# The end of the down projection: a turned tile copied between its sums, PSUM copies between squares, the fourth Winograd sum ahead of the corner

## The reference, cut to what matters

```python
for i in range(DEPTH):                       # DEPTH = 2
    u = rms_norm_2(h, mix_pre_g[i])
    # layer 0: dilated attention, layer 1: differential attention; both begin with u @ w_in
    h = h + rms_norm_2(y, mix_post_g[i])
    # ... attention to a memory, in the same form ...
    u = rms_norm_2(h, ffn_pre_g[i])
    y = swiglu_ffn(u, w_gate_up[i], w_down[i])       # (silu(g) * up) @ w_down
    h = h + rms_norm_2(y, ffn_post_g[i])

def rms_norm_2(x, g):
    y = xf * lax.rsqrt(jnp.mean(xf * xf, axis=-1, keepdims=True) + EPS)
    return (y * g).astype(x.dtype)
```

## Time and profile before

| | us |
|---|---|
| median of 3 runs | 3115.54 |
| lowest, highest | 3115.42, 3120.82 |
| profiled execution, its own time | 3113.84 |
| its span | 3112.0 |
| PE busy in the span | 2887.1 (93%) |
| DVE busy | 1111.0 (36%) |
| ACT busy | 667.3 (21%) |
| POOL busy | 508.7 (16%) |

### The profile page before, as it was taken

How to read it: one execution, slowest core, us unless ns; L and a number is a source line. 1 busy time by engine, 2 the same in 40 slices (tenths; PEclk the granted TensorE clock), 3 DMA queues, 4 the chain that set the end, 5 groups by cost and what they waited for, 6 DMA issues and landing times.

```text
span 3112.0 us, 32431 instructions
## 1 busy us (share of the span) xinstructions
PE 2887.1 (93%) x12564; PEld 1910.6 (61%) x12564; DVE 1111.0 (36%) x2286; ACT 667.3 (21%) x1512; POOL 508.7 (16%) x777
## 2 busy tenths in 40 slices
PE   8999998889999987899999999999798899999998
PEld 4465543244655432387656488888585554688887
DVE  3534311135343111334621243354346722333354
ACT  3332210023232100102621211100204622211100
POOL 2001111121021111112310012100113610011201
PEclk9999999999999999999999999999899999999999
DMA  3113599941116999622021122222121021122122
GB/s 146 48 48 148 211 394 410 415 168 48 48 64 225 388 417 414 243 82 81 1 79 57 54 82 82 82 75 102 54 82 55 1 81 54 54 85 106 68 75 88
DMA packets 121906, 421.35 MB, mean 135 GB/s; under 512 B 9232, under 2 KB 13456, under 8 KB 95504
## 3 DMA queue, kind: packets, MB, share of 16 engines
q1 hardware_dynamic: 108528, 383.62, 32.3%
q0 software_dynamic: 12640, 33.45, 2.9%
q10 hardware_dynamic: 576, 2.10, 0.2%
HBM read 408.64 MB, written 27.26 MB: 140 GB/s over the span
## 4 chain that ended last, share of the span: by engine, by line
PE 79%; DMA 10%; DVE 4%; ACT 2%; issue 2%; DVEq 1%; POOLq 0%; POOL 0%; SPq 0%; ACTq 0%
PE ps L2359 31%; PE ps L406 13%; DMA ring_feat<-in_w 7%; PE ps L2593 6%; PE ps L1591 4%; PE ps L1071 4%; PE ps L2613 4%; PE ps L1631 2%; PE ps L2467 2%; PE ps L2839 2%; DMA big<-in_w 2%; PE ps L1843 1%; PE ps L1854 1%; PE ps L1866 1%; PE ps L2684 1%
## 5 line engine op out<-in xcount | busy, mean ns | idle before, releaser
L406 PE MATMUL ps<-ring_feat 128*96 128x512 f32 (+3 forms) x768 | 308.5, 558 | 11.0 <-DVE tmp L465 4.4
L2359 PE MATMUL ps<-big 128*128 128x256 f32 x1200 | 268.1, 379 | 0.0
L2359 PE MATMUL ps<-ring_feat 128*128 128x256 f32 x1152 | 262.3, 379 | 0.0
L2359 PEld LDWEIGHTS ps<-big 128*128 128x128 f32 x1200 | 228.0, 190 | 31.0
L406 PEld LDWEIGHTS ps<-ring_feat 128*128 128x128 f32 (+1 forms) x768 | 140.6, 186 | 163.6 <-issue 122.1
L2359 PEld LDWEIGHTS ps<-ring_feat 128*128 128x128 f32 x1152 | 218.9, 190 | 30.6 <-issue 1.0
L2593 PE MATMUL ps<-ring_feat 128*128 128x512 f32 x448 | 194.6, 593 | 2.9 <-ACT ring_feat L2739 2.2
L1591 PE MATMUL ps<-big,tmp 128*64 128x512 f32 x512 | 123.7, 632 | 33.7 <-DMA big<-in_w 30.7
L1591 PE MATMUL ps<-ring_feat,tmp 128*64 128x512 f32 x512 | 123.8, 632 | 28.4 <-DMA ring_feat<-in_w 26.4
L2593 PEld LDWEIGHTS ps<-ring_feat 128*128 128x128 f32 x448 | 84.2, 190 | 106.7 <-issue 101.9
L1606 DVE TENSOR_TENSOR tmp<-tmp,ps 128x256 f32<-128x256 f32 x32 | 13.5, 421 | 328.0 <-ACT tmp L1600 328.0
(11 more groups left out here) (467 smaller groups left out, 4506.4 us busy)
## 6 DMA issues: line engine op xcount, KB each, us to landing
big<-in_w SPq DMA_DIRECT2D x48, 2048.0 KB, 17.5
ring_feat<-in_w SPq DMA_DIRECT2D x48, 2048.0 KB, 14.9
ring_feat<-in_w_gate_up SPq DMA_DIRECT2D x22, 2048.0 KB, 8.0
ring_feat<-in_w_mix_in SPq DMA_DIRECT2D x12, 2048.0 KB, 8.1
ring_feat<-in_w_down SPq DMA_DIRECT2D x12, 1536.0 KB, 6.7
tmp<-in_w_mem_kv SPq DMA_DIRECT2D x6, 2048.0 KB, 20.5
ring_feat<-in_w_out SPq DMA_DIRECT2D x4, 2048.0 KB, 8.6
big<-expert_out SPq DMA_DIRECT2D x16, 512.0 KB, 7.9
```

The source lines that it names most:

```text
L406: yield T.matmul(bank, lhs(k), rhs(k), start=k == 0, stop=k == n - 1)
L2359: m = T.matmul(to, lhs[:, j, :], rhs[:, j, :], start=start and j == 0, stop=stop and j == chunks - 1)
```

## The change

The last read-out of the down projection is written in another order, and one POOL sum changes place.

In the Winograd sums (both `mix_group` and the down projection) U4 comes ahead of C22 on POOL. U4 is now written over U2 where it was written over P5, so that C22 can still read P5; the drain between the two is gone. DVE's corner C12 reads U4 there. Waits for the last of POOL's sums name C22 now.

`down_read` and the calls of `add_tile` become one function, `down_outputs`, that writes each engine's list for both groups. In the first half nothing but U4's place is different. In the second half:

```diff
+            if name == "act":
+                copy_plain(0)
+                copy_outer(0)
+                square(0)
+                copy_plain(1)
+                if half:
+                    entry(0, x_square)
+                copy_outer(1)
+                if half:
+                    entry(0, x_scale)
+                    entry(1, x_square, x_scale)
+                square(1)
+                if half:
+                    entry(2, x_square)
+                    entry(3, x_square)
+                    entry(2, x_scale)
+                    entry(3, x_scale)
+            if name == "dve":
+                inner(0)
+                corners(0)
+                if half:
+                    add(0)
+                    add(1)
...
+                inner(1)
+                if half:
+                    entry(0, x_turn)
+                corners(1)
+                if half:
+                    entry(1, x_turn)
+                    add(2)
+                    add(3)
...
+            if name == "pool":
+                outer(0)
+                if half:
+                    y_roots(0)
+                    entry(0, x_root)
+                outer(1)
+                if half:
+                    entry(1, x_root)
+                    y_roots(1)
+                    entry(2, x_root)
+                    entry(3, x_root)
```

`copy_plain` is the copy of P1, `copy_outer` those of P7 and P5, `inner` C11 and U2, `corners` C12 and C21, `outer` POOL's three sums. `entry` does its steps only where another layer follows; `x_square`, `x_root`, `x_scale` and `x_turn` are the steps of the next layer's norm. `add` is the multiplication with the gain and the addition to h:

```diff
+            def add(t):
+                gain(t)
                 eng.drain()
+                eng.wait_ge(y_root, y0 + t + 1 - 2 * LAYERS * TT)
+                V.scalar_tensor_tensor(out=x[:, t, :], in0=buf[:, t, :], scalar=y_ss(y0 + t)[:, 0:1], in1=x[:, t, :],
+                                       op0=ALU.mult, op1=ALU.add).then_inc(x_added, 1)
...
             if nxt is not None:
...
+                if name != "dve":
+                    turn_x(name, eng, 0)
+                    turn_x(name, eng, 1)
...
                 G.tensor_tensor(out=p7_, in0=p7_, in1=u2, op=ALU.add).then_inc(outer_added, 1)
                 eng.drain()
+                G.tensor_tensor(out=u2, in0=p5_, in1=u2, op=ALU.add).then_inc(outer_added, 1)
                 G.tensor_tensor(out=out[:, g + 2, HI], in0=p7_, in1=p5_, op=ALU.add).then_inc(outer_added, 1)
-                eng.drain()
-                G.tensor_tensor(out=p5_, in0=p5_, in1=u2, op=ALU.add).then_inc(outer_added, 1)
```

More of the change, by code:

```diff
@@ L2978, in down_group, with down_outputs, parts, copy_plain @@
                 m4.then_inc(up_full, 1)
[L2980 to L2985, removed]
+        def down_outputs(name, eng, l, half, sets, end, buf, post, y0, j0, nxt):
             cols = slice(half * 512, (half + 1) * 512)
             low, high = slice(half * 512, half * 512 + 256), slice(half * 512 + 256, (half + 1) * 512)
-            if name == "act":
+            def parts(g):
+                return (2 * half + g, *d_staged[4 * g:4 * g + 4], *split_banks(sets[g]))
+            def copy_plain(g):
+                n, p1_, p7_, p5_, u2, first, second = parts(g)
                 if half:
-                    eng.wait_ge(outer_added, g_pool("down", l, n - 2, D_U4))
+                    eng.wait_ge(outer_added, g_pool("down", l, n - 2, D_C22))
                     eng.wait_ge(hidden_ready, g_dve("down", l, n - 2, D_C21))
@@ L2993, in down_read, with copy_outer @@
                 A.activation(p1_, first[0], ACT.Copy).then_inc(silu_ready, 1)
+            def copy_outer(g):
+                n, p1_, p7_, p5_, u2, first, second = parts(g)
                 eng.wait_ge(up_full, g_full("down", l, n, D_FULL["P7_P5"]))
@@ L3015, in down_read, with gain, outer @@
                 eng.wait_ge(outer_added, g_pool("down", l, n, D_U4))
[L3016 to L3021, removed]
+                V.tensor_tensor(buf[:, 2 * g, high], u2, second[3], ALU.add).then_inc(hidden_ready, 1)
+                V.tensor_tensor(buf[:, 2 * g + 1, low], p7_, first[3], ALU.add).then_inc(hidden_ready, 1)
+            def gain(t):
+                eng.wait_ge(silu_ready, g_act("down", l, 2 * half + t // 2, D_SQUARE + t % 2))
+                V.tensor_tensor(buf[:, t, cols], buf[:, t, cols], post[:, cols], ALU.mult)
+            def outer(g):
+                n, p1_, p7_, p5_, u2, first, second = parts(g)
                 eng.wait_ge(hidden_ready, g_dve("down", l, n, D_U2))
@@ new lines, in down_outputs @@
+            if name == "dve":
[4 more added lines that the diff above has]
+                    add(1)
+                else:
+                    gain(0)
+                    gain(1)
+                inner(1)
[6 more added lines that the diff above has]
+                    add(3)
+                else:
+                    gain(2)
+                    gain(3)
@@ L3062, in down_projection @@
                 if slot % 4 == 3:
[L3063 to L3067, removed]
+                    if half and nxt is not None:
+                        late[name] = (j0, buf, nxt)
+                    down_outputs(name, eng, l, half, sets, ends[slot], buf, post, y0, j0, nxt)
                 slot_done(name)
             if nxt is not None:
-                late[name] = (j0, buf, nxt)
                 if name == "pe":
```

52 lines of the change are left out of this document (37 added, 15 removed).

## The result

The changed kernel took 3098.19 us in the median of 4 runs (3097.02 to 3099.36), the kernel before beside it 3115.56: a ratio of 0.9938, with a 95% interval of 0.9926 to 0.9950. In a second comparison, on another occasion, the median of 6 runs was 3097.54 and the ratio 0.9942 (0.9928 to 0.9956). The profiled execution took 3097.71 with a span of 3095.9. The forecast was 3097.5.

What follows compares the result with a forecast made beforehand. PE, busy 93% of the span, was taken as the bound, so only its waits could pay. Seam 14.5, mixer ends 1.75 and tail 1.8 make 18.05 us off the median 3115.54: 3097.5, range 3093 to 3103.

Steps and rivals of the forecast that it cites:

- What PE waited for at the seam: Between down projection and next layer's first product, PE waits 12.2 us for DVE's turned copy L338; this wait would go.
- The rival in which PE finds another wait and keeps its 12 us: At the seam, another wait replaces L338's; only 3.6 us gained elsewhere, time 3112.0; chance 0.05.
- C12 0.8 earlier, by U4's new place: Group 0's corner on DVE at the seam starts at about 2177.2 in place of 2178.02, 0.8 us gained.
- Tile 1's addition and the root beside it: At the seam, tile 1's root on POOL ends near 2182.4; DVE adds tile 1 from 2182.5 to 2183.8.
- Tile 0's scaling, covered: At the seam, ACT scales tile 0 until 2185.8; its transposes start at 2186.06 as before, with 0.25 us of cover.
- Tile 1's scaling is last: At the seam, ACT's scaling of tile 1 ends last, at 2189.2; PE transposes it then in place of 2190.58.
- The product and the clock: Seam gain of 13.5 to 16.0 us, depending on whether PE's clock stays high; 14.5 taken as the middle.
- The rival of a clock that falls after the turn began: Half clock for 6 us behind the seam's turn costs 3.0 us: seam 13.0, time 3099.0; chance 0.16.
- The tail: After PE's last product, the read-out gains 1.8 us, with bounds 1.0 and 2.2.
- The mixer ends: At the end of the mixer's passes in both layers, PE's wait shrinks by 0.87 us each, 1.75 together.
- The signs: Signs of being right: first product 4 to 5 us behind last matmul, L338 and tail corners within 0.3, second wait 1.5 to 2.5.
- A root of more than 2 us on POOL: Named as a sign of being wrong, anywhere in the changed profile; no chance of its own.

Runs made afterwards that it cites:

- e3: The changed kernel with DVE's turned copies of tiles 0 and 1 put back behind tile 3's addition; 3105.45 us, 0.9962 of the kernel before.
- e4: The kernel before with only DVE's turned copies moved early, tile 0's behind tile 1's addition, tile 1's behind group 1's corners; 3107.81 us, ratio 0.9969.
- e1: The kernel before with only POOL's sums swapped, U4 ahead of C22 and written over U2; 3110.97 us, 0.9980 of the kernel before.
- e2: The changed kernel with POOL's old order of sums, the new lists otherwise kept; 3102.83 us, 0.9954 of the kernel before.
- e8: The changed kernel with two extra 128x512 matmuls on PE between the two turns, results never read; 3095.87 us, 0.9932 of the kernel before.
- c: The changed kernel run once more, beside the kernel before, in a second comparison; 3097.54 us, 0.9942 of the kernel before.
- e7: e5 with DVE's gains of both tiles ahead of both additions again; 3096.24 us, 0.9932 of the kernel before.
- e5: The changed kernel with tile 1's transposes on PE moved into the middle of tile 0's product; 3096.79 us, 0.9938 of the kernel before.

## Why the prediction was right

**What PE waited for at the seam.** Right. The 12.2 us were the place of L338 in DVE's list and what stood ahead of it. e3 brings 6.4 of them back by that place alone; in e4, with the old lists, the same move leaves a wait of 2.9, now for C21. The rival in which PE finds another wait and keeps its 12 us holds for no run; in e4 there is another wait, but a short one.

**C12 0.8 earlier, by U4's new place.** Right: 0.82 at the seam and 0.88 at each mixer end (2.60 to 1.72, and 2.6 to 1.7), in seven traces with the swap against three without. e1 shows the swap alone: 4.85 by its pieces.

**Tile 1's addition and the root beside it.** The step was mis-sized. I had L306 shut out for the addition alone, as in the earlier trace rows, and only L308 beside the gain; together the root of tile 1 was to end 5.2 behind C12. It ended 5.5 behind it (2182.18 less 2176.68): L306 took 1.91, through the addition and the gain that follows it without a gap. That costs 0.3 at tile 1's addition. At the seam the 0.25 of cover of tile 0's scaling took up nearly all of it.

**Tile 0's scaling, covered.** Right but for 0.09. L304 took 1.31 beside the addition, and the turn started 1.38 behind the last row of products in place of 1.29; the cover of 0.25 was used up by the root's 0.3, and e2 shows that nothing of it is left. The Trainium skill's rule is that two SBUF inputs on DVE shut out a GpSimd instruction that reads SBUF (page "SBUF — State Buffer", section "Who interferes with whom"). The 1.31 agree with it, and so do the 0.22 that the same L304 took at 2186.66 beside the turned copy, which reads PSUM.

**Tile 1's scaling is last.** Right. It was to end 3.1 behind the first turn and ended 3.16 behind it (2187.63 + 1.15 less 2185.62); PE's wait of 2.15 was forecast as 2.1.

**The product and the clock.** I took 14.5 from 13.5 to 16.0 and it was 14.4. That it lay within 0.1 is partly luck: 14.5 was the middle between a clock that falls before the turn and one that does not fall, and in the changed kernel it fell within the turn. Stretches of the changed kernel show that:

```profile
2186.70:2188.80 2.10, 0.00 (x0) 0.00 (x0) 1.95 (x4) 1.17 (x2) 0.75 (x2) 1.00 0.74 193
2188.80:2190.50 1.70, 1.67 (x9) 1.67 (x10) 0.00 (x0) 1.31 (x4) 0.86 (x2) 0.62 1.05 406
2190.50:2193.00 2.50, 2.50 (x4) 0.96 (x4) 2.41 (x4) 0.00 (x0) 0.87 (x3) 0.57 1.03 391
2193.00:2205.20 12.20, 12.20 (x30) 5.29 (x29) 3.34 (x4) 4.48 (x6) 2.12 (x4) 1.00 0.01 2
```

The turn took 1.65, between 1.04 and 1.93, and two tiles 14.9, of 13.7 at the upper level. e8 puts the two losses together at 1.68, against 1.8 expected. The rival of a clock that falls after the turn began comes nearest; its half clock of 6 us was 3.4 here, with 6.2 in e4's tiles (3.2 lost). The place of the fall is not fixed by the pause. It came 0.4 us into tile 1's turn here, 0.8 into it in c, just behind the turn in e3 with the same pause of 2.15, and 0.65 ahead of it in e2 with a pause of 2.33. Whether the transposes themselves count for the clock no run here separates.

**The tail.** The term was mis-sized: 1.42 for 1.8, within its bounds of 1.0 to 2.2. Both errors are the root again. Group 0's chain is later by 0.3, of which U2 and so U4 take 0.2 (C12 at 1.71 behind the last product's row, not 1.52); and the last root takes 1.91, so that the last addition starts 5.53 behind C12, not 5.3. e1, with the old order of gains, has a tail 0.29 shorter; e7 confirms it in the new lists.

**The mixer ends.** Right: 1.76 for 1.75, and PE's wait for C22 cost nothing: C22 ends at 1449.03, before C21 at 1449.19.

**The median.** 18.05 was forecast, 17.6 is the sum of the pieces, 17.4 and 18.9 are what two comparisons gave. The executions of one kernel scatter by more than these differ, so the closeness of the medians says less than that of the pieces.

**The signs.** The product starts 4.57 behind the end of the last matmul (2190.27 less 2185.70), L338 0.04 behind the first transposes, C12 in the tail 0.25 behind PE's last product, and PE's second wait is 2.15: all as named. One sign of being wrong was badly set. A root of more than 2 us on POOL did occur: L306 and L308 together took 2.62 (2179.56 to 2182.18). But the prediction's own working had 2.4 for that root, so the sign would have shown even with every step as forecast.

## What to carry to other kernels

A long wait behind an engine that is busy 36% of the time is a matter of that engine's list: look at what stands ahead of the awaited instruction and whether it could stand behind. Such a move pays in full only if the next wait in the same place is moved too, here the one for the corners; ask of each step what PE would meet next. Where two sums leave an engine one after the other, put the one that someone waits for first; here a drain went as well. And where several reorderings go in together, test each: the alternating gains were part of the change and cost 0.3 us.

## What the hardware showed that I had not expected

A small POOL instruction (L306, one element a partition, 0.30 us alone) took 1.39 beside one DVE addition with its two SBUF inputs, and 1.91 beside an addition and a gain that follow each other. It ended 0.08 us behind the gain's end, so here the waiting instruction did not get its turn between the two. e7, which parts the pair, has the 1.39 again.

After the pause of 2.1 us ahead of tile 1's turn both traces of the changed kernel show the lower clock, from within the turn on. A pause of 1.5 us (e5 and e7), or one of 2.15 with 1.7 us of matmuls in it (e8), left the clock at 1.00. That is two traces and one; as the fall came as early as 1.7 us after the end of tile 0's turn in e2, and as late as 3.9 after it in e4, they do not show that it never comes in such a pause. The price here was 1.7 us for 3.4 us at the lower level.
